# Pooling, attention and two expert layers on one core: a rearranged transition to attention, residuals by halves, and another order for VectorE

## The reference, cut to what matters

```python
cs = jax.nn.silu(c)
for i in range(DEPTH):
    mod = (cs @ ada_w[i] + ada_b[i])[:, None, :]
    sh1, sc1, g1, sh2, sc2, g2 = jnp.split(mod, 6, axis=-1)
    hm = x * (1.0 + sc1) + sh1
    if i % N_MIXERS == 0:
        y = multiscale_pool_mixer(hm, pool_w_in[j], pool_w_grp[j], pool_scale[j], pool_w_out[j])
    else:
        y = dilated_attention_mixer(hm, attn_w_in[j], attn_w_out[j])
    x = layer_norm(ALPHA * x + (1.0 + g1) * y, ln1_g[i], ln1_b[i])
    hf = x * (1.0 + sc2) + sh2
    y = moe_ffn(hf, router_w[i], router_b[i], exp_w_gu[i], exp_w_down[i], sh_w_gu[i], sh_w_down[i])
    x = layer_norm(ALPHA * x + (1.0 + g2) * y, ln2_g[i], ln2_b[i])
```

## Time and profile before

| | |
|---|---|
| runs without profile | 1567.44, 1576.07, 1579.24 us, median 1576.07 |
| the profiled execution | 1576.43 us, its span 1574.7 us |
| busy share of the span | PE 92%, PEld 55%, DVE 36%, ACT 26%, POOL 5% |
| chain that ended last | PE 78%, DVE 14%, issue 3%, ACT 2%, DMA 2% |
| granted TensorE clock, mean | 0.967 |
| moved by DMA | 522.17 MB, mean 332 GB/s |

### The profile page before, as it was taken

How to read it: one execution, slowest core, us unless ns; L and a number is a source line. 1 busy time by engine, 2 the same in 40 slices (tenths; PEclk the granted TensorE clock), 3 DMA queues, 4 the chain that set the end, 5 groups by cost and what they waited for, 6 DMA issues and landing times.

```text
span 1574.7 us, 19309 instructions
## 1 busy us (share of the span) xinstructions
PE 1448.9 (92%) x7546; PEld 866.5 (55%) x7546; DVE 572.2 (36%) x1098; ACT 404.2 (26%) x617; POOL 72.6 (5%) x48
## 2 busy tenths in 40 slices
PE   6999999999999999579998988779999999999995
PEld 2544544545545455379897987644445455454452
DVE  0574222222222222666646564461222222222224
ACT  1222212112121121324445444341121121221212
POOL 0001200000000000230000000021000000000001
PEclk9999999999999999779999997889999999999998
DMA  9994999999999999847244432176999999999990
GB/s 392 424 426 159 374 416 427 424 427 427 425 426 411 421 422 395 347 145 285 108 188 164 185 111 77 71 310 252 422 427 425 425 417 422 420 412 421 416 390 27
DMA packets 50513, 522.17 MB, mean 332 GB/s; under 512 B 5633, under 2 KB 5889, under 8 KB 8225
## 3 DMA queue, kind: packets, MB, share of 16 engines
q1 hardware_dynamic: 48512, 514.61, 79.2%
q0 software_dynamic: 1952, 6.88, 1.2%
HBM read 520.42 MB, written 1.05 MB: 331 GB/s over the span
## 4 chain that ended last, share of the span: by engine, by line
PE 78%; DVE 14%; issue 3%; ACT 2%; DMA 2%; SPq 0%; DVEq 0%; ACTq 0%
PE psum L1374 28%; PE psum L1399 15%; PE psum L1331 8%; PE psum L1322 5%; PE psum L1427 4%; PE psum L1428 4%; PE psum L1429 4%; DVE modulation_sums L843 2%; PE psum L1229 2%; DVE slots_of_tokens L1045 2%; DVE slice_parts L432 2%; PE psum L1308 2%; DVE slots_T L1070 2%; DVE scores L1127 1%; PE psum L1515 1%
## 5 line engine op out<-in xcount | busy, mean ns | idle before, releaser
L1374 PE MATMUL psum<-weights,slots_of_tokens 128*64 128x512 f32 x2048 | 452.2, 592 | 0.0
L1374 PEld LDWEIGHTS psum<-weights,slots_of_tokens 128*64 128x64 f32 x2048 | 175.7, 137 | 263.9 <-issue 263.9
L1399 PE MATMUL psum<-weights,hidden_T 128*64 128x512 f32 x1024 | 233.8, 597 | 12.1 <-DVE slot_weight L1074 12.1
L1080 DVE SCALAR_TENSOR_TENSOR slot_rows<-psum,slot_weight,slot_rows 128x512 fp32r<-128x512 f32 x128 | 96.1, 751 | 243.7 <-ACT slot_rows L755 243.7
L1066 DVE TENSOR_TENSOR hidden<-gate,psum 128x256 f32<-128x256 f32 x64 | 27.0, 421 | 374.8 <-ACT gate L747 374.8
L1322 PE MATMUL psum<-slot_matrix,h_parts 128*128 128x512 f32 x576 | 157.5, 399 | 0.0
L1399 PEld LDWEIGHTS psum<-weights,hidden_T 128*64 128x64 f32 x1024 | 80.8, 136 | 136.3 <-issue 136.3
L1427 PE MATMUL psum<-h_transposed_high,slice_parts 128*128 128x256 f32 x384 | 114.0, 297 | 35.4 <-DVE slice_parts L432 21.8
L1331 PE MATMUL psum<-slot_rows,slots_T 128*128 128x512 f32 x528 | 139.7, 406 | 3.8 <-DVE slot_rows L1080 3.8
L1331 PEld LDWEIGHTS psum<-slot_rows,slots_T 128*128 128x128 f32 x528 | 93.9, 188 | 74.9 <-issue 57.4
L747 ACT ACTIVATE gate<-psum 128x256 f32<-128x256 f32 x64 | 24.6, 384 | 410.2 <-PE psum L1374 410.2
(11 more groups left out here) (174 smaller groups left out, 1382.2 us busy)
## 6 DMA issues: line engine op xcount, KB each, us to landing
weights<-in_exp_w_gu SPq DMA_DIRECT2D x128, 2048.0 KB, 13.5
weights<-in_exp_w_down SPq DMA_DIRECT2D x128, 1024.0 KB, 10.8
weights<-in_attn_w_in SPq DMA_DIRECT2D x36, 1024.0 KB, 5.2
weights<-in_ada_w SPq DMA_DIRECT2D x16, 2048.0 KB, 12.2
slots_of_tokens<-in_ada_w SPq DMA_DIRECT2D x7, 2048.0 KB, 10.1
weights<-in_pool_w_in SPq DMA_DIRECT2D x2, 2048.0 KB, 25.6
weights<-in_pool_w_out SPq DMA_DIRECT2D x2, 2048.0 KB, 21.0
weights<-in_sh_w_gu SPq DMA_DIRECT2D x2, 2048.0 KB, 9.4
```

The source lines that it names most:

```text
L1080: V.scalar_tensor_tensor(yw[:, 1, c], PS[:, BD + half, :], wslot[:, 0:1], yw[:, 0, c].bitcast(F32), ALU.mult, ALU.subtract).then_inc(lo.yl, 1)
L1374: last = mm(PS[j * SLOTS:(j + 1) * SLOTS, BGU, :], XgT[ob][:, k, s0:s0 + SLOTS], gu_w(ws + j)[:, k, :], start=k == 0, stop=k == KD - 1, ti ...
L1399: last = mm(PS[j * SLOTS:(j + 1) * SLOTS, BD + half, :], HT[:, k, j * SLOTS:(j + 1) * SLOTS], dn_w(ws + j)[:, k, half * HALF:(half + 1) * ...
```

## The change: what it does

- **Accumulators and banks.** Two more accumulators for slices below 16 (`more_modulation_sums`, in free phase memory; `sums(n)`), and banks 6, 7, 4, 5 for slices 12 to 15, so that four slices are under way at a time.
- **Residual by halves.** `y_ready` counts halves (banks of 512 columns) instead of tiles; `residual(n, t, b)` does one half, `variance` the rest. In norms 1 to 3 `deviation` of tile 0 comes after the first half of tile 1. ScalarE loads the square root's table ahead by an operation on an unused column (`load_sqrt`).
- **Expert loop.** VectorE does `slots_T` and `slot_weight` ahead of `slots_dve`.
- **Transition.** All four `ada` in a row; low parts of slices 0 and 1 on VectorE instead of GpSimd; the transposes write h in token order (32 elements apart in PSUM), ScalarE scales columns 0 to 3 of each tile and VectorE 4 to 7; the first projection waits for three of the four quarters of h; slice 1 is made after h.
- **Attention.** The accumulation of slices 16 and 17 stands behind weight slices 6 to 9, that of 18 to 23 in two heads each of heads 0 to 11; low parts of slices 36 to 39 stand behind the scores of head 12 and in heads 12 to 14.
- **Pool mixer.** Sums of slices 6 and 7 after tile 0's products, 8 and 9 after tile 1's; in norm 0's experts, `ada(11)` stands behind the second transposes.

```diff
         def sum_bank(n):
-            return 6 + n % 2 if n < 16 else 5
+            return 5 if n >= 16 else (6, 7, 4, 5)[n - 12] if n >= 12 else 6 + n % 2
+        def bank_read(n):
+            return n if n >= 16 else 0 if n < 2 else min(n - 1, 12)
+        def sums(n):
+            return acc[:, n % 2, :] if n >= 16 or n % 4 < 2 else more_sums[:, n % 4 - 2, :]
+        def sums_free(n):
+            return max(16, n - 1) if n >= 16 else max(0, n - 3)
...
         def gemv_of_head(hb, hh):
-            return {(0, 1): (19, 0), (0, 2): (19, 1), (1, 0): (20, 0), (1, 1): (20, 1), (1, 2): (21, 0), (1, 3): (21, 1),
-                    (2, 0): (22, 0), (2, 1): (22, 1), (2, 2): (23, 0), (2, 3): (23, 1)}.get((hb, hh))
+            return (18 + (hb * HB + hh) // 2, hh % 2) if hb < BATCHES - 1 else None
...
-            for n in range(2):
-                pool.wait_ge(w_hi, n + 1)
-                slice_lower(G, n)
...
+            load_sqrt()
             ada_copy(12)
+            slice_high(0)
             ada_copy(13)
             norm(1, (0,))
             ada_copy(14)
-            slice_high(0)
+            ada_copy(15)
             norm(1, (1,))
-            ada_copy(15)
-            slice_high(1)
+            act.wait_ge(sum_read, 16)
             for t in range(TT):
+                act.wait_ge(hT_mm, 8 + 2 * t + 1)
+                for k in range(4):
+                    last = nc.scalar.activation(tmp[:, t, k * P:(k + 1) * P], hT_chunk(2, t, k), ACT.Identity,
+                                                bias=shiftc[:, 2, k:k + 1], scale=scale[:, 2, k:k + 1])
+                last.then_inc(h_act, 1)
...
+            slice_high(1)
...
-            def residual(n, t):
...
+            def residual(n, t, b):
+                y = PS[:, mixer_bank(n, t) + b, :]
+                c = slice(b * HALF, (b + 1) * HALF)
+                count = 2 * TT * n + 2 * t + b + 1
+                dve.wait_ge(y_ready, count)
+                V.tensor_tensor(y, y, gate[:, n % 2, c], ALU.mult).then_inc(y_read, 1)
+                dve.wait_ge(y_read, count)
+                step(V.scalar_tensor_tensor(tmp[:, t, c], x[:, t, c], ALPHA, y, ALU.mult, ALU.add))
+                step.settle()
+                step(V.bn_stats(stats[:, t, b], tmp[:, t, c]))
...
                             V.tensor_tensor(hx[:, :], sg[:, :], PS[:, BGU, HID:2 * HID], ALU.mult).then_inc(lo.h, 1)
-                            dve.wait_ge(lo.fill, n * 2 + 9)
-                            slots_dve(1 - i // 4, 2 * (i % 4), BG).then_inc(lo.copy_dve, 1)
                             dve.wait_ge(lo.tr, n + 1)
...
                             last.then_inc(lo.PT, 1)
+                            dve.wait_ge(lo.fill, n * 2 + 9)
+                            slots_dve(1 - i // 4, 2 * (i % 4), BG).then_inc(lo.copy_dve, 1)
...
                 elif hh == HB - 1:
                     head_scores(h + 1)
+                    if hb == BATCHES - 2:
+                        slice_low(9 * BATCHES)
...
+                    chunk = hT_chunk(m, t, k)
+                    if m == 2:
+                        chunk = chunk.rearrange("p (r i) -> p i r", r=4)
+                    last = nc.tensor.transpose(chunk, x[:, t, k::KD], ident)
...
-                ada_sum(7 + 2 * t)
+                for n in (6 + 2 * t, 7 + 2 * t):
+                    ada_sum(n)
...
-            ada(12)
-            ada(13)
+            for n in range(12, 16):
+                ada(n)
             ada_sum(12)
             ada_sum(13)
-            ada(14)
             transpose_h(2, 0)
             ada_sum(14)
-            ada(15)
+            ada_sum(15)
             transpose_h(2, 1)
-            ada_sum(15)
```

More of the change, by code:

```diff
@@ L931, in norm @@
                         dve.wait_ge(x_ready[t], n)
-                residual(n, 0)
-                deviation(n, 0)
+                residual(n, 0, 0)
+                residual(n, 0, 1)
+                variance(n, 0)
+                if n == 0:
+                    deviation(n, 0)
+                    ada_final(6)
+                    ada_final(7)
+                    residual(n, 1, 0)
+                else:
+                    residual(n, 1, 0)
+                    deviation(n, 0)
+                residual(n, 1, 1)
+                variance(n, 1)
                 if n == 0:
                     ada_final(8)
-                if n == 1:
-                    ada_final(12)
-                    ada_final(13)
-                residual(n, 1)
-                if n == 0:
                     ada_final(9)
                 deviation(n, 1)
-                if n == 1:
-                    ada_final(14)
             def route(L):
@@ L1091, in _, with slice_low @@
             norm(1)
-            ada_final(15)
+            def slice_low(n):
+                if n < SLICES:
+                    dve.wait_ge(w_hi, n + 1)
+                    slice_lower(V, n)
+            slice_low(0)
+            for n in range(12, 16):
+                ada_final(n)
             dve.wait_ge(sum_read, 16)
             for t in range(TT):
-                for half in range(2):
-                    dve.wait_ge(hT_mm, 8 + 2 * t + half + 1)
-                    for k in range(4 * half, 4 * half + 4):
-                        last = V.tensor_scalar(tmp[:, t, k * P:(k + 1) * P], hT_chunk(2, t, k), scale[:, 2, k:k + 1], shiftc[:, 2, k:k + 1],
-                                               ALU.mult, ALU.add)
-                    last.then_inc(h_ready, 1)
+                dve.wait_ge(hT_mm, 8 + 2 * t + 2)
+                for k in range(4, 8):
+                    last = V.tensor_scalar(tmp[:, t, k * P:(k + 1) * P], hT_chunk(2, t, k), scale[:, 2, k:k + 1], shiftc[:, 2, k:k + 1],
+                                           ALU.mult, ALU.add)
+                last.then_inc(h_ready, 1)
                 for half in range(2):
@@ L1197, in ada_sum @@
                     pe.wait_ge(ada_acc, ON_DVE.index(n) + 1)
[L1198 removed]
+                if bank_read(n):
+                    pe.wait_ge(sum_read, bank_read(n))
                 one = cst[:, C_SEL:C_SEL + 1] if on_pe else cst[:, C_ONE:C_ONE + 1]
                 if ada_slice[n][1] in (G1, G2):
[L1201 removed]
+                    mm(PS[:, sum_bank(n), :], one.broadcast_to([P, P]), sums(n), start=True, stop=True).then_inc(sum_mm, 1)
                     return
                 for k in range(4):
[L1204 removed]
+                    last = mm(PS[:, sum_bank(n), k:k + 1], sums(n)[:, k * P:(k + 1) * P], one, start=True, stop=True)
                 last.then_inc(sum_mm, 1)
@@ L1276, in _ @@
                                   start=k == 0, stop=k == KD - 1)
-                    if t and half == 0:
-                        ada_sum(8)
-                last.then_inc(y_ready, 1)
-                ada_sum(7 + 2 * t)
+                    last.then_inc(y_ready, 1)
+                for n in (6 + 2 * t, 7 + 2 * t):
+                    ada_sum(n)
             def moe(L):
@@ L1332, in scatter @@
                                           start=False, stop=True, skip_group_check=True)
-                        if done is not None:
-                            last.then_inc(done, 1)
+                            if done is not None:
+                                last.then_inc(done, 1)
                 pe.wait_ge(lo.P, 1)
```

114 lines of the change are left out of this document (55 added, 59 removed).

## The result

The changed kernel takes 1534.98 us (median of four runs, 1533.0 to 1540.74) against 1577.39 for the kernel before: ratio 0.9746, 95% interval 0.9703 to 0.9788. In a second measurement it took 1534.9 (six runs, 1534.22 to 1536.9; ratio 0.9761, 0.9728 to 0.9794). The forecast was 1535, in a range of 1524 to 1552. The profiled execution took 1533.0.

The account below looks back on a forecast made before the run. The prediction took TensorE, busy 92% of the span, as the bound, with the transfers next. Its terms summed to -41.3 us, so 1576.4 becomes 1535, in a range of 1524 to 1552.

Parts of the forecast that it names:

- Loops: Both expert loops, 64 pairs: VectorE's new order lets TensorE start down projections 0.32 us earlier a pair; -19.5 us.
- My 1.0 for the transfers: Expert loops: 1.0 us taken off the gain because the transfer rate might be a little too low.
- Transition: Last scatter to first projection: slices off GpSimd, residual by halves, h scaled on both engines; -15.5 us (10 to 17).
- For h I took 6.5: Transition, scaling of h to first projection: 6.5 us instead of 9.95, between 5.8 and 7.1.
- Projections: First projections: accumulations moved to slices 6 to 9 avoid GpSimd's gain, slice 3 late by 1; -6.0 us (-3 to -8).
- Heads 0 to 11: Attention heads: two accumulation halves move into heads 0 and 3 and make slices late; +2.9 us (1 to 6).
- Heads 12 to 15: Last heads: two slices move behind head 12's scores, removing a 4.15 us wait, part taken back; -2.5 us (0 to -5).
- Pool mixer: Before the first expert loop: shorter residual left and transposes not behind a waiting condition product; -2.0 us (-0.5 to -4).
- Norms 2 and 3: Later norms and the output's chain: deviation 0.7 us later, the halves' saving waited away; +1.3 us (-2 to +3).
- B: Rival, expert loops: transfers already set the pace, the 19.5 us goes to nothing, 1554.5 us; chance 0.12.
- C: Rival, transition: the transposes' scattered PSUM write is slow, 16 cost 12 us more, 1543 us; chance 0.06.
- D: Rival, expert loop: the moved slot copy comes late for the next pair's products, whole gain gone or 1599 us; chance 0.02.

Follow-up runs that it names:

- a2: Changed kernel, but every second gather in the expert loop leaves out the low part of h (2 of its 4 matmuls): 1526.27 us, one run.
- again: Profiled execution of the second measurement of the unaltered changed kernel; that measurement's median was 1534.9 us.
- d1: Kernel before, with slices 0 and 1 lowered on VectorE instead of GpSimd and slice 1 made behind h: 1566.29 us, ratio 0.9932.
- a4: Changed kernel, but the transposes ahead of the attention write in order and h's high and low parts are read with a stride: 1541.86 us.
- b3: Changed kernel, with the halves of the modulation sums back in slices 2 to 7 of the projections and in their old heads: 1542.8 us.
- b2: Changed kernel, with the residual done by whole tiles again instead of by halves: 1538.26 us.
- a1: Kernel before, with only the expert loop's order changed: VectorE takes slots_T and slot_weight ahead of its slot copy. 1552.77 us, ratio 0.9842.
- b4: Changed kernel, with tile 0's deviation ahead of tile 1's first residual half in norms 1 to 3: 1537.91 us, one run.
- a3: Changed kernel, but each load of down-projection weights in the expert loop brings only its first half: 1539.04 us, one run.

## Why the prediction was right, point by point

- **Loops, -19.5 forecast, -17.1 measured.** The mechanism stood; the size failed at one step. I ended the pair by VectorE's chain (1.00 us from the second gather's start) and let TensorE be free after 0.91, "as the first did". a2 shows the chain at 1.01 us, so that was well read, but the second gather needs 1.07 itself. 1.32 less 1.07 is 0.25 a pair where I had 0.32, and 0.27 was measured. My 1.0 for the transfers was wrong too: nothing was to be taken off. The lower bound, the wait of 0.19 as counted, was too low: 0.27 came, more than the wait that the profile counts.
- **Transition, -15.5 and -14.8 (-15.7 again).** From the first half of the residual to the scaling I had 14.3 us. VectorE's row L936 starts at 626.63 and the last `h_shift` ends just before the scaling, 14.7 later:

```profile
626.63 0.70 DVE L936 TENSOR_TENSOR psum<-psum,gates 128x512 f32<-128x512 f32 x1 [0.37 <-PE psum L1368]
...
641.14 0.16 DVE L906 TENSOR_TENSOR h_shift<-psum,h_shift 128x4 f32<-128x4 f32 x1
641.34 1.50 ACT L795 ACTIVATE residual_or_h<-psum,h_shift,h_scale 128x128 f32<-128x128 f32 x4 [2.93 <-DVE h_shift L906]
...
647.79 0.55 PE L1462 MATMUL psum<-h_transposed_high,slice_parts 128*128 128x256 f32 x1 [5.07 <-DVE h_transposed_low L1142]
```

  The two tiles with their deviations take 10.4 us of it (9.4 and 0.8 in the forecast), slice 0 2.2, the results 2.1 with a wait of 0.47 for TensorE's last sum, and that wait is the 0.4 more than I had. The other 0.25 are the first half's early start: it doesn't come, VectorE begins 1.54 us after the last scatter as before (1.50). For h I took 6.5; it is 6.45. That GpSimd's first subtraction cost 4 us was right in kind (d1), and a4 gives the interleave 2.1.
- **Projections, -6.0 and -7.8.** The long step of 12.94 us became 6.68, 6.26 less: slice 3 is late by 0.9 as foreseen, at 3.84 us. b3 confirms the cause. What my sum lacked is two other steps of before, where TensorE ran a modulation sum between projections; ScalarE's copies of the results show one, and after has none:

```profile
711.56 0.60 ACT L785 ACTIVATE qkv<-psum 128x512 f32<-128x512 f32 x1 [3.37 <-PE psum L1429]
718.16 0.60 ACT L785 ACTIVATE qkv<-psum 128x512 f32<-128x512 f32 x1 [4.21 <-PE psum L1429]
```

  6.60 us instead of 5.76, twice, is 1.7 more.
- **Heads 0 to 11, +2.9; +2.5 in after, +5.4 again.** The waits moved as forecast: for slices from 21.1 us in ten to 23.6 in eleven, for the transposes from 0.6 to 1.1, together 3.0. The eleven waits are 2.1 us each on average, as the forecast's 2.2. Eight traces with these heads have 225.5 to 232.9, mean 230.3; five with the old ones 223.0 to 226.5, mean 225.0. At the same mean granted clock in the heads, 0.970, one with the new ones has 229.9 and three with the old ones 226.0 to 226.5. So the edit costs some 4 to 5, inside the forecast's 1 to 6, and the +2.5 of after is low for it: its heads ran at 0.978, those of again, with the same waits, at 0.963.
- **Heads 12 to 15, -2.5 and -4.3.** The wait of 4.15 us for the scores became 0.59, but the softmax behind it waits 3.3 us where it waited 1.2; all waits of the stretch together fall by 1.1 only (14.8 to 13.7). The rest goes with the clock (0.90 instead of 0.80): TensorE is busy 3.1 us less with the same work. The forecast had no term for it. The stretch in before, then in after (us, busy, instructions, granted clock, share and rate of transfers):

```profile
962.90:1016.60 53.70, 38.87 (x235) 0.80 0.02 5
```

```profile
932.40:981.80 49.40, 35.75 (x236) 0.90 0.03 6
```

- **Pool mixer, -2.0 and -1.96**, of which b2 gives the halves about 1.3. The other part, the transposes ahead of condition product 11, depends on how long that product waits for its weights. In a1, whose code is that of before up to the loop, it waited longer than the 2.05 us of the earlier trace rows, and the first pair came at 155.04 us and not 151.71:

```profile
113.65 3.64 PE L1188 MATMUL psum<-slots_of_tokens,condition_repeated 128*32 128x512 f32 x16 [4.37 <-DMA slots_of_tokens<-in_ada_w]
```

  In the eleven traces with the new start it came at 149.6 to 151.1. So the stage as a whole gains 2 us against the trace of before and 4 to 5 against that of a1.
- **Norms 2 and 3, +1.3 and 0.0 (+2.7 again, with the lower clock of the last section).** b4 shows no cost of the deviation's place. The end grew by 0.6 us (19.50 to 20.07) and norm 2 gave as much back; why is open.
- **The rivals.** B (a1, a3), C (a4) and D (a1) are refuted for this kernel. By the Trainium skill's 425 GB/s the loops would have given an estimated 16 us, nearer to the 17.1 than my 19.5, but a3 shows that the reason was another.

That the forecast came out within 0.1 us of the median is luck. The traces differ by 43.5 us and not 41.3: loops and transition gave 3.1 us less than forecast, projections and heads 12 to 15 gave 3.6 more with terms that I hadn't seen, and a single execution of the changed kernel lies anywhere in 1533 to 1541.

## What to carry to other kernels

A one-column VectorE operation on the path is worth protecting from a GpSimd subtraction like these: 0.16 us became 4.27 and 3.30, and taking the two subtractions off GpSimd gave 7 us in VectorE's timeline and 8 to 9.5 in the times. When a wait is removed, compute the next bound for every engine that takes part in the handover, with the duration of that very operation; here the neighbour's 0.91 instead of its own 1.07 cost 3 us of the forecast. Where TensorE transposes anyway, try to let it do the permutation too: here it was free, and the strided reads of the other engines had cost 2 us.

## What the runs showed of the hardware

Within one kernel the times fall into groups by granted clock. In 37 runs of the kernel before that went with the experiments, nine took 1564.7 to 1567.5 us at a mean clock of 0.974 to 0.976, the others 1573.5 to 1579.8 at 0.964 to 0.970. a1 gives 1547.7 and 1548.0 at 0.977, 1557.6 and 1562.3 at 0.966 to 0.967. The changed kernel was nine times in ten at 0.973 to 0.977. At the higher clock in both it is 32 us faster and not 42: part of the gain between medians goes with more executions at the higher clock. Whether the change brings that about, by its shorter idle stretches, is not shown. Where the kernel before gains its 10 us at the higher clock stays open, since none of those runs was profiled.

In the traces the same work shows at two paces. Sixteen products of the shared expert after norm 2, first in after, then in again:

```profile
1006.09 7.08 PE L1345 MATMUL psum<-weights,h_transposed 128*128 128x512 f32 x16
```

```profile
1007.92 8.57 PE L1345 MATMUL psum<-weights,h_transposed 128*128 128x512 f32 x16
```

TensorE had waited for the norm before both; in the second the clock was still at 1.2 GHz for part of them (mean 0.81 between 992 and 1036 us, 0.86 in after), and the stage took 46.1 us instead of 44.0. An edit worth under 5 us can't be judged by the median of four such runs; the stages of the traces say more, if the clock of each is read beside them.
